# Six of the shared expert's eight sums move from VectorE to ScalarE and GpSimd

## The reference, cut to what matters

```python
x = layer_norm(ALPHA * x + mix, ln1_g, ln1_b)          # x1
scores = sigmoid(x1 @ router_w)                          # picks 8 of 64 experts per token
routed = sum over the chosen experts of gate * swiglu(x1, w_gate[e], w_up[e], w_down[e])
shared = swiglu(x1, sh_gate, sh_up, sh_down)
out = layer_norm(ALPHA * x1 + routed + shared, ln2_g, ln2_b)
```

## Time and profile before

| | |
|---|---|
| runs | 2023.01, 2015.5, 2017.63 us; median 2017.63 |
| the profiled execution's own time | 2019.8 us |
| its span in the trace | 2018.1 us |
| PE busy | 1937.1 us (96%) |
| DVE, ACT, POOL busy | 1114.9, 762.3, 546.8 us |
| mean granted clock of TensorE | 0.985 |

### The profile page before, as it was taken

The page is one execution under the profiler, slowest core; times in us unless marked ns, Lnnn a source line. Parts: engine busy times, 40 slices in busy tenths (PEclk is TensorE's granted clock), DMA queues, the critical chain, the costliest instruction groups (busy, mean ns, idle before and its releaser), DMA issues.

```text
span 2018.1 us, 38544 instructions
## 1 busy us (share of the span) xinstructions
PE 1937.1 (96%) x12659; PEld 1680.8 (83%) x12659; DVE 1114.9 (55%) x3378; ACT 762.3 (38%) x1495; POOL 546.8 (27%) x894
## 2 busy tenths in 40 slices
PE   8999999999999999999999899999999999999991
PEld 8778889888988778888787779889888889998981
DVE  6735563655366553232657755555555556666654
ACT  3424551554244541111544023333344434333344
POOL 7365565000023300000100224334444442222210
PEclk9999999999999999999999989999999999999996
DMA  4521312212333521110331489999999999999995
GB/s 170 119 78 53 85 48 74 64 48 58 95 102 107 144 63 47 47 47 16 130 138 63 155 293 294 332 307 316 324 332 325 325 324 374 366 374 341 347 338 197
DMA packets 173655, 376.35 MB, mean 186 GB/s; under 512 B 24725, under 2 KB 115765, under 8 KB 148721
## 3 DMA queue, kind: packets, MB, share of 16 engines
q1 hardware_dynamic: 147568, 307.82, 42.2%
q0 software_dynamic: 25408, 67.16, 14.7%
q10 hardware_dynamic: 576, 0.05, 0.0%
HBM read 322.29 MB, written 63.14 MB: 191 GB/s over the span
## 4 chain that ended last, share of the span: by engine, by line
PE 36%; DMA 11%; DVE 2%; ACT 1%; issue 1%; DVEq 0%; POOLq 0%; POOL 0%; SPq 0%; ACTq 0%
PE ps_gu L2763 17%; DMA scr_acc<-y_main,out_idx 8%; PE ps_wo L92 2%; PE ps_ye L92 2%; PE ps_wo L93 2%; PE ps_wo L94 2%; PE ps_ye L94 2%; PE ps_ye L93 2%; DMA w_raw<-in_exp_w_up 2%; PE ps_gu L2732 2%; PE ps_ye L2779 2%; DMA x_main<-scr_x,idx 1%; PE ps_xt L2740 0%; ACT x_main L2984 0%; PE ps_xt L1933 0%
## 5 line engine op out<-in xcount | busy, mean ns | idle before, releaser
L2763 PE MATMUL ps_gu<-xe,w_raw 128*128 128x136 f32 (+7 forms) x4096 | 504.4, 284 | 1.8 <-DMA w_raw<-in_exp_w_up 1.8
L2763 PEld LDWEIGHTS ps_gu<-xe,w_raw 128*128 128x128 f32 x4096 | 492.5, 191 | 2.6 <-DMA w_raw<-in_exp_w_up 2.3
L2705 POOL DMA_INDIRECT scr_acc<-y_main,out_idx x64 | 99.5, 1555 | 276.2 <-DMA scr_acc<-y_main,out_idx 147.4
L1192 ACT ACTIVATE w_raw_first<-w_raw_first,o_stage 128x128 f32<-128x128 f32 (+1 forms) x192 | 86.4, 450 | 199.4 <-DVE o_stage L1138 198.6
L2882 DVE TENSOR_TENSOR w_lo<-w_raw,w_hi 128x1024 fp32r<-128x1024 f32 x128 | 150.5, 1217 | 2.2 <-ACT w_hi L2814 2.2
L2814 ACT ACTIVATE w_hi<-w_raw 128x1024 fp32r<-128x1024 f32 x128 | 128.0, 1048 | 32.2 <-DMA w_raw<-in_exp_w_down 32.1
L2852 ACT ACTIVATE y_main<-ps_ye,gate 128x512 f32<-128x512 f32 (+2 forms) x128 | 88.0, 688 | 114.8 <-PE ps_ye L94 114.8
L2699 POOL DMA_INDIRECT scr_acc<-y_rest,out_idx x38 | 66.8, 1759 | 216.4 <-ACT y_rest L2846 202.8
L2907 DVE TENSOR_TENSOR e_h<-e_silu,ps_gu 128x128 f32<-128x128 f32 (+7 forms) x128 | 37.4, 292 | 152.6 <-PE ps_gu L2763 152.6
L2834 ACT ACTIVATE e_silu<-ps_gu 128x128 f32<-128x128 f32 (+7 forms) x128 | 36.0, 281 | 208.5 <-PE ps_gu L2763 208.5
L92 PE MATMUL ps_ye<-w_hi,e_h_hi 128*128 128x512 f32 (+2 forms) x256 | 106.9, 418 | 0.2 <-DVE e_h_lo L2911 0.2
(11 more groups left out here) (517 smaller groups left out, 4690.3 us busy)
## 6 DMA issues: line engine op xcount, KB each, us to landing
w_raw<-in_exp_w_gate SPq DMA_DIRECT2D x64, 1024.0 KB, 9.2
w_raw<-in_exp_w_up SPq DMA_DIRECT2D x64, 1024.0 KB, 7.9
w_raw<-in_exp_w_down SPq DMA_DIRECT2D x64, 1024.0 KB, 8.2
w_raw_first<-in_w_in SPq DMA_DIRECT2D x24, 512.0 KB, 4.7
v_w_raw<-in_w_in SPq DMA_DIRECT2D x48, 256.0 KB, 2.7
scr_att<-o_stage SPq DMA_DIRECT2D x16, 264.0 KB, 2.9
att_prev<-scr_att SPq DMA_DIRECT2D x16, 264.0 KB, 4.2
merged<-in_x_cols SPq DMA_DIRECT2D x8, 512.0 KB, 8.0
```

Source lines behind the costliest of these rows:

```text
L1192: act.activation(probs[:, w % 2, 0:n], probs[:, w % 2, 0:n], ACT.Exp, scale=-1.0, bias=o_stage[:, blk, at + 1:at + 2], accum_out=o_stage[: ...
L2705: pool.indirect_dma_start(out=acc_rows[0], out_offset=bass.IndirectOffsetOnAxis(ap=out_idx[j][0:rows, 0:1], axis=0), in_=y_main[j][0:rows, ...
L2763: ins = pe.matmul(ps_gu[:, 2 * w + c, 0:width], w3(raw[j][w])[:, k, P * c:P * c + P], xT[:, k, 0:width], start=(k == 0), stop=(k == KD - 1))
```

## The change: what it does

Shares 0 and 1 stay on VectorE. For shares 2 to 7 ScalarE copies the PSUM area into the `acc` tile. GpSimd then multiplies the x1 tile by ALPHA in place, and adds it to the `acc` tile. TensorE waits for the copy now, SyncE for GpSimd's sum. ScalarE's copy into a tile that is used again (shares 4 to 7) waits until the store of its first share has landed. GpSimd does shares 2, 3 and 4 between the gathers of item 0 and item 1, and 5, 6 and 7 after them. TensorE's `sums(1)` moves from behind `down(3)` to behind `down(4)`.

```diff
+        BY_DVE = 2
+        it.share_copied, it.copied_shares = share_copied, NT - BY_DVE
+        released = lambda s: (acc_ready, s + 1) if s < BY_DVE else (share_copied, s + 1 - BY_DVE)
+        summed_at = lambda s: (acc_ready, s + 1) if s < BY_DVE else (share_summed, s + 1 - BY_DVE)
+        acc_free = lambda s: [(acc_out[acc_at(s)], 16)] if s >= 4 else []
+        back_loaded = lambda s: (ld_back[slot_at(s)], 16 * (s // 4 + (1 if slot_at(s) >= 2 else 0)))
...
             for i in range(NT):
-                sp.wait_ge(acc_ready, i + 1)
+                sp.wait_ge(*summed_at(i))
                 sp.dma_start(acc_d[:, SHARES[i], :], acc[acc_at(i)]).then_inc(acc_out[acc_at(i)], 16)
...
-            for n in range(2):
-                it.gather(pool, n, n, CAP)
+            def add_share(s):
+                pool.wait_ge(share_copied, s + 1 - BY_DVE)
+                pool.wait_ge(*back_loaded(s))
+                rows = by_row(acc[acc_at(s)])
+                pool.tensor_scalar(by_chunk(back[slot_at(s)]), by_chunk(back[slot_at(s)]), ALPHA, None, ALU.mult).then_inc(share_scaled, 1)
+                pool.wait_ge(share_scaled, s + 1 - BY_DVE)
+                pool.tensor_tensor(rows, by_chunk(back[slot_at(s)]), rows, ALU.add).then_inc(share_summed, 1)
+
+            it.gather(pool, 0, 0, CAP)
+            for s in range(BY_DVE, 5):
+                add_share(s)
+            it.gather(pool, 1, 1, CAP)
+            for s in range(5, NT):
+                add_share(s)
...
                 if s >= 2:
-                    pe.wait_ge(acc_ready, s - 1)
+                    pe.wait_ge(*released(s - 2))
...
                 down(s)
-                if s == 1 or s == 3:
-                    it.sums(pe, ps_it, s // 2, CAP)
+                if s == 1 or s == 4:
+                    it.sums(pe, ps_it, s // 3, CAP)
...
+            for s in range(BY_DVE, NT):
+                act.wait_ge(dn_done, s + 1)
+                for sem, value in acc_free(s):
+                    act.wait_ge(sem, value)
+                act.activation(acc[acc_at(s)], ps_s[:, 2 * (s % 2):2 * (s % 2) + 2, :].rearrange("p h n -> p (h n)"),
+                               ACT.Copy).then_inc(share_copied, 1)
...
             it.select(dve, chi, 0, CAP)
-            add_share(0)
-            add_share(1)
+            for s in range(BY_DVE):
+                add_share(s)
             it.indices(dve, chi, ps_it, 0, 0)
             it.select(dve, chi, 1, CAP)
-            add_share(2)
-            add_share(3)
             it.indices(dve, chi, ps_it, 1, 1)
             it.select(dve, chi, 2, CAP)
-            for s in range(4, NT):
-                add_share(s)
...
-                pe.wait_ge(it.shares, NT - 1)
+                pe.wait_ge(it.share_copied, it.copied_shares - 1)
                 pe.wait_ge(it.idx_made, 2)
                 turn_rows(0, 1, CAP)
                 turn_more(0, 0, 1)
-                pe.wait_ge(it.shares, NT)
+                pe.wait_ge(it.share_copied, it.copied_shares)
```

More of the change, by code:

```diff
@@ L2028, in project_and_route @@
                  "ld_rows", "turned", "x_hi", "x_lo", "ld_r", "ld_b", "ld_d", "r_hi", "r_lo", "sh_hi", "sh_lo",
-                 "logits_done", "logits_copied", "r_done", "score", "mask", "pos_done", "cnt_done", "over", "place_done",
+                 "logits_done", "logits_copied", "r_done", "score", "mask", "share_copied", "share_scaled", "share_summed", "pos_done", "cnt_done", "over", "place_done",
                  "place_ready", "tab_done", "tab_ready", "gates", "pieces", "gu_done", "silu", "h", "h_hi", "h_lo", "dn_done", "acc",
@@ L2033, in project_and_route @@
          ld_rows, turned, x_hi_made, x_lo_made, ld_r, ld_b, ld_d, r_hi_made, r_lo_made, sh_hi_made, sh_lo_made,
-         logits_done, logits_copied, r_done, score_ready, mask_ready, pos_done, cnt_done, over_ready, place_done,
+         logits_done, logits_copied, r_done, score_ready, mask_ready, share_copied, share_scaled, share_summed, pos_done, cnt_done, over_ready, place_done,
          place_ready, tab_done, tab_ready, gates_ready, pieces_made, gu_done, silu_made, h_made, h_hi_made, h_lo_made, dn_done, acc_ready,
@@ L2041, in project_and_route @@
         acc_out = it.acc_out
-        it.shares = acc_ready
+        BY_DVE = 2
[4 more added lines that the diff above has]
+        back_loaded = lambda s: (ld_back[slot_at(s)], 16 * (s // 4 + (1 if slot_at(s) >= 2 else 0)))
         ident = cst["ident"]
@@ L2540, in add_share @@
                 dve.wait_ge(dn_done, s + 1)
[L2541 to L2546, removed]
+                dve.wait_ge(turned, 2 * NT)
                 dve.scalar_tensor_tensor(out=by_row(acc[acc_at(s)]), in0=by_chunk(back[slot_at(s)]), scalar=ALPHA,
```

## The result

The changed kernel takes 2049.66 us (median of 4 runs, 2046.93 to 2050.61) against 2019.12 us (2015.5 to 2023.01) for the kernel before, measured beside it: a ratio of 1.0147, 95% interval 1.0135 to 1.0159, or 29.7 us with 27.3 to 32.1 (the two medians themselves are 30.5 us apart). Its profiled execution spans 2047.7 us.

A forecast was written before the change was run, and what follows sets the result against it. TensorE, 96% busy, was taken as the bound, waiting for VectorE's late sums. Item 1 17.0 us later plus 2.8 us of low clock gave 19.8 on 2019.8, 2039.6; less 2.2 to the median, 2037.5 us, range 2031 to 2045.

The forecast's parts named there:

- six shares, 6S: GpSimd's scaling and addition for shares 2 to 7, S us a share: S 5.6, bounds 3.9 to 7.2.
- gather 1, gaps, the port: GpSimd's other time before its last sum: gather 1 at 4.0 us, gaps and VectorE holding the port at 2 us.
- last sum to ScalarE's copy of DOWN: From GpSimd's last sum through SyncE's issue of item 1's weights and the DMA to ScalarE's copy: 11.7 us.
- ScalarE's spare: ScalarE waits 1.30 us for TensorE's transposed rows before item 1, so 1.3 us of lateness is absorbed.
- item 1's rows on ScalarE later by: Start of item 1: last sum 18.3 us later, less ScalarE's 1.3 us, makes 17.0 us.
- one more stretch at the lower clock: TensorE stands still over 3.54 us once more, then runs a stretch at granted clock 0.50: 2.8 us.
- The step that failed: Pricing a share on GpSimd at 5.6 us, middle of 3.9 and 7.2, with the strided scaling at 3.3 at most.
- SyncE's queue as the way of the delay: Item 1's three matrices stay queued behind share 7's store, so the late last sum delays item 1 by 17.0 us.
- The ring hidden, the front gains nothing: Four `acc` tiles: share 4's copy waits for share 2's store, `down(6)` starts no earlier; front gains 0 us, further delay hidden.
- The port as a second, hidden lateness: Rival, 0.13: GpSimd holds VectorE; item 0's product near 1199, hidden, or work ends at 1207, adding 2 us; up to 2042.
- The rivals of cheap sums: GpSimd's sums cost 3.9 us a share, shift 8.8 us, 2026.4 us, no effect told; chance 0.14.
- GpSimd in time: Rival: last sum by 1175.1, needing S of 2.8 us a share; 2012.3 us at best; chance 0.05 together.

The follow-up runs named there:

- experiment 5: Changed kernel with GpSimd's scaling reading x1 stepped but writing flat into a free tile, so the addition has no stepped operand from it; its total time is not stated.
- experiment 8: Changed kernel and kernel before, each run and traced again unaltered; medians stayed within 1.3 us, the two ratios of the medians giving 29.7 and 31.3 us.
- experiment 1: Changed kernel with item 1's three weight matrices issued behind the store of share 3, not share 7; the median fell by 9.3 us.
- experiment 4: Changed kernel with shares 4 and 5 in two further free tiles, so ScalarE's copies of them wait for no store; time unchanged.
- Experiments 1 and 3: Changed kernel with item 1's weights issued early: alone, median 9.3 us lower; together with GpSimd's scaling run flat through its tile, 2031.0 us.
- experiment 6: Changed kernel with ScalarE scaling the x1 tiles and GpSimd only adding: ratio 1.0009 to the kernel before; with item 1's weights early as well, 2023.56 us.
- experiment 7: Only shares 4 to 7 off VectorE, scaling on ScalarE; and kernel before with `select(2)` after sums 4 to 7, alone and with weights early: all within 0.1% of before.

## Why the prediction was wrong

The direction, the path and the place were right; 2049.7 us lies above the range. Its terms, each measured against the first trace of before and with the lag of 2.26 us taken off:

```
term                                         forecast      measured
first share begins on GpSimd                 1152.5        1152.6
six shares, 6S                               33.6          45.2
gather 1, gaps, the port                     6.0           4.2
last sum ends                                1192.1        1202.0
last sum to ScalarE's copy of DOWN           11.7          11.3
ScalarE's spare                              -1.3          -1.3
item 1's rows on ScalarE later by            17.0          26.46
one more stretch at the lower clock          2.8           2.35
item 0's first products done in the wait     -             -1.47
total                                        19.8          27.3
```

- **The step that failed** is "I take 5.6, the middle ... and the scaling is nearer to the copy than to the cast", with "3.3 at most" behind it. The scaling was priced at no more than 3.3 us and took 4.65. Read afterwards, the cast of the earlier trace rows, 1.40 us for 512 elements, is the flat scaling's 2.8 us, and VectorE's factor 1.64 of the earlier trace rows times 2.8 is 4.6. I had put this factor on the addition's high end and not on the scaling's. That it fits may be chance: experiment 5 shows GpSimd's cost of the step as 0.9 us for each stepped operand of the scaling and 0.5 us for that of the addition. The addition, 2.9 us, lay in its bounds of 2.4 to 3.9. S was 7.5 and its high end 7.2, and this alone is 11.6 us. The gather and the gaps gave 1.8 us of it back.
- **The Trainium skill's figures** ("GPSIMD Engine Reference", section 7) would have given 2.5 us for the scaling, 3.6 for the addition. These are estimates from that page; the trace, with 4.65 and 2.9 us, agrees with neither. Their sum of 6.1 errs to the same side as my 5.6.
- **The clock's term was about right:** 2.35 us in place of 2.8. From 1200 to 1210 the granted clock was 0.50 and TensorE did item 0's first products in 3.64 us instead of 1.93, but ScalarE still waited for the weights and hid that. Behind ScalarE's rows the clock was low again: the twelve matmuls that follow took 5.17 us (1218.71 to 1223.88) in place of 2.82 (1191.46 to 1194.28), and they lie on the path. What the sum left out is a gain: in the kernel before, item 0's first products lie between ScalarE's rows and these matmuls, here they were done in the wait, so the matmuls begin 1.24 us behind the rows and not 2.71. Windows of the changed kernel:

```profile
1200.00:1210.00 10.00, 3.64 (x32) 1.58 (x32) 7.04 (x14) 0.00 (x0) 4.18 (x2) 0.50 0.49 174
...
1220.00:1225.00 5.00, 5.00 (x37) 3.81 (x37) 0.30 (x3) 1.37 (x2) 3.18 (x2) 0.63 1.01 388
```

- **The base, not settled.** The last 2 to 3 us (27.3 by the traces, 29.7 by the ratio) would fit the trace of before that I did not have, with its stretch of 57.3 us, but its longer lag speaks against it (experiment 8). The prediction took the 2.8 us of slow clock in its one trace for a fixed part of the kernel. Another 1.5 us are in the median of before, 2017.63 over three runs and 2019.12 over four.
- **SyncE's queue as the way of the delay: right,** and shown by experiment 1 for the last 11 us; without it the other 16 come by VectorE. Nothing was given back: right.
- **The ring hidden, the front gains nothing: right,** by experiment 4. The removed waits of 1.60 and 1.07 us bought nothing. With only shares 4 to 7 moved the removed 3.54 us bought nothing either; with the scaling on ScalarE a wait of 5.01 us stands in its place.
- **The port as a second, hidden lateness: right in kind.** TensorE had the product at 1206.09, 1203.8 without the lag, between the 1199 and the 1207 of that rival's two cases, and ScalarE's rows released it only at 1218.37. Experiments 1 and 3 show VectorE as the bound once the weights are out of the way. The rivals of cheap sums and of GpSimd in time are out by S; experiment 6, where 2.9 us a share gives the time of before, agrees with the 2.8 us at which the latter was to decide.

## What to carry to other kernels

Price an operation that moves to another engine by the row nearest to it in kind on that engine (here the cast came nearer than the copy), give every stepped operand its own surcharge, and leave room above the range where no row shows the operation itself; where it needs no order, write it flat, or let the engine with the cheap row do it. Look at what stands behind the moved work in a queue: item 1's weights needed nothing from the sums, and issuing them four stores earlier took back 9 of the 30 us. Before a wait seen in one trace is booked as a gain, look at a second execution: two traces of the same kernel had 3.54 and 0.81 us of it and put the fall of the clock at different waits, and the three kernels of experiment 7, in which it was 1.07 us or less, took the time of before.

## What the runs showed of the hardware

- GpSimd, 128x1024 f32 in SBUF: scaling 2.8 us flat, 3.7 with its input at a step of 512 bytes, 4.65 with the output stepped as well; addition 2.4 flat, 2.9 with one stepped input. ScalarE scales the same tile flat in 1.05 us.
- Two GpSimd additions in a row held one VectorE selection for 6.38 us. In the changed kernel the 18 instructions of VectorE's last selection before item 0's product took 12.1 us (1192.69 to 1204.79) instead of 3.4 (1184.65 to 1188.10). There VectorE got one instruction in between GpSimd's addition (1193.85 to 1196.70) and scaling (1196.67 to 1201.29), and in the middle of the scaling five more at their usual length:

```profile
1193.83 2.96 DVE L1923 TENSOR_SCALAR e_sel<-e_slots,e_place 128x256 bf16<-128x256 bf16 x1
1196.70 1.91 DVE L1925 TENSOR_SCALAR e_sel_more<-e_slots_more,e_place 128x128 bf16<-128x128 bf16 x1
1198.54 0.28 DVE L1923 TENSOR_SCALAR e_sel<-e_slots,e_place 128x256 bf16<-128x256 bf16 x1
...
1199.45 1.89 DVE L1925 TENSOR_SCALAR e_sel_more<-e_slots_more,e_place 128x128 bf16<-128x128 bf16 x1
```

- The Trainium skill, "SBUF — State Buffer", section "Who interferes with whom", says that the engine which issues first holds the port pair for its whole instruction. The trace agrees for GpSimd's additions, which held VectorE for 2.9 us each; it does not for GpSimd's scaling, which held it for 1.9 us, let it work for some 0.9 us and held it for 1.9 us again. The measurement decides.
- The fall of the granted clock to 0.50 in this stretch came behind the waits of 1.6 and 1.0 us in one execution of the kernel before and behind the wait of 3.5 us in another, with 2.9 us between their stretches, a lag of 2.13 us ahead of the shorter one, and 0.2 us between their spans. Why it does so is not shown, nor where the lag of up to 3.8 us before the stretch comes from; it appears in steps in code that no run changed.
